# Prompt-tile heads issued one tile ahead, and a reordered end of the sample tile, in a hybrid DeltaNet / mLSTM encoder step

## What is computed

```python
# gated DeltaNet, per head, chunk by chunk
A = eye + where(strict, beta * (k @ k.T) * gam, 0)          # gam: decays between tokens
u_v, w = solve(A, [beta * v, beta * exp(G) * k])            # unit lower triangular
u = u_v - w @ S
o = exp(G) * (q @ S) + ((q @ k.T) * gam) @ u
S = exp(gL) * S + k_end.T @ u
o_a = o * rsqrt(mean(o * o) + EPS) * gdn_norm_w * silu(z_a)
# mLSTM, per head: stabilised, h = num / max(|den|, exp(-m))
h_b = h * rsqrt(mean(h * h) + EPS) * mlstm_norm_w * sigmoid(o_b)
x = x + concat([o_a, h_b]) @ w_out
```

## Time and profile before

| | us |
|---|---|
| median of 3 runs | 2611.95 (2611.59 to 2615.35) |
| the profiled execution | 2611.51, its span 2609.8 |
| PE busy in the span | 2564.2 (98%) |
| DVE busy | 2105.4 (81%) |
| ACT busy | 1213.3 (46%) |
| GpSimd busy | 355.2 (14%) |
| granted TensorE clock, mean | 0.995 |

### The profile page before, as it was taken

One profiled execution on the slowest core, in us unless ns is written; L12 is line 12 of the kernel. 1 busy time (PEld: TensorE's weight loads), 2 busy tenths in 40 slices (PEclk: granted clock), 3 DMA queues, 4 the chain that ended last, 5 costly groups with the idle time before them and its releaser, 6 DMA issues.

```text
span 2609.8 us, 43704 instructions
## 1 busy us (share of the span) xinstructions
PE 2564.2 (98%) x17600; PEld 2533.9 (97%) x17600; DVE 2105.4 (81%) x2614; ACT 1213.3 (46%) x1921; POOL 355.2 (14%) x186
## 2 busy tenths in 40 slices
PE   9999999998999999999999999999999999999998
PEld 9999999998999799999999999999999999999998
DVE  7979786887787889898877998988757788898756
ACT  5535454343444545455445554645311355454445
POOL 2200003332010120000024200000333300000042
PEclk9999999999999999999999999999999999999999
DMA  4223323232114423223323222223322222332231
GB/s 127 82 81 92 87 78 90 61 84 78 53 36 111 130 65 90 82 82 91 88 71 94 71 83 81 82 85 91 88 77 74 61 78 81 90 89 82 84 97 49
DMA packets 420251, 215.13 MB, mean 82 GB/s; under 512 B 19218, under 2 KB 418011, under 8 KB 420048
## 3 DMA queue, kind: packets, MB, share of 16 engines
q1 hardware_dynamic: 406066, 205.36, 27.6%
q10 hardware_dynamic: 13982, 6.96, 1.0%
HBM read 204.58 MB, written 7.68 MB: 81 GB/s over the span
## 4 chain that ended last, share of the span: by engine, by line
PE 56%; DVE 8%; ACT 2%; issue 1%; POOL 0%; DVEq 0%; ACTq 0%
PE ps L1124 13%; PE ps L1126 13%; PE ps L1125 13%; PE ps L1109 5%; PE ps L1110 5%; PE ps L1113 5%; PE ps L1182 1%; PE ps L1184 1%; PE ps L1183 1%; DVE sumsq L2666 1%; DVE ut L2561 1%; DVE x L3389 1%; DVE tau_lo L2630 1%; DVE r L2752 0%; DVE x L3574 0%
## 5 line engine op out<-in xcount | busy, mean ns | idle before, releaser
L1057 POOL TENSOR_TENSOR wlo<-raw,whi 128x1024 fp32r<-128x1024 f32 (+2 forms) x150 | 339.7, 2266 | 2215.9 <-ACT whi L1852 2215.9
L1124 PE MATMUL ps<-tau_hi,whi 128*128 128x320 f32 x1280 | 396.2, 309 | 0.5 <-ACT sq L2090 0.5
L1125 PE MATMUL ps<-tau_lo,whi 128*128 128x320 f32 x1280 | 395.9, 309 | 0.0
L1126 PE MATMUL ps<-tau_hi,wlo 128*128 128x320 f32 x1280 | 395.9, 309 | 0.0
L1863 ACT CAST whi<-raw 128x512 fp32r<-128x512 f32 (+4 forms) x368 | 258.1, 714 | 195.3 <-PE ps L1126 189.3
L1109 PE MATMUL ps<-xh,whi 128*128 128x320 f32 x1040 | 317.0, 313 | 4.2 <-POOL wlo L1057 2.3
L1110 PE MATMUL ps<-xl,whi 128*128 128x320 f32 x1040 | 313.4, 309 | 0.0
L2577 DVE TENSOR_TENSOR wlo<-raw,whi 128x512 fp32r<-128x512 f32 (+4 forms) x368 | 289.4, 801 | 17.3 <-ACT whi L1863 17.1
L1109 PE MATMUL ps<-hh,whi 128*128 128x320 f32 x928 | 282.4, 312 | 4.4 <-DVE hl L3018 2.1
L1110 PE MATMUL ps<-hl,whi 128*128 128x320 f32 x928 | 280.3, 310 | 0.0
L2577 DVE TENSOR_TENSOR wlo<-wsum,whi 128x1536 fp32r<-128x1536 f32 (+2 forms) x112 | 180.8, 1614 | 81.8 <-ACT whi L1863 80.3
(11 more groups left out here) (498 smaller groups left out, 6120.0 us busy)
## 6 DMA issues: line engine op xcount, KB each, us to landing
raw<-in_ffn_w_gu SPq DMA_DIRECT2D x320, 256.0 KB, 3.8
raw<-in_ffn_w_d SPq DMA_DIRECT2D x96, 192.0 KB, 3.0
raw<-in_w_in_even SPq DMA_DIRECT2D x32, 512.0 KB, 4.1
raw<-in_ffn_w_d SPq DMA_DIRECT2D x32, 384.0 KB, 3.6
raw<-in_w_in_odd SPq DMA_DIRECT2D x24, 512.0 KB, 3.8
raw<-in_ffn_w_gu SPq DMA_DIRECT2D x16, 512.0 KB, 4.3
raw<-in_ffn_w_d SPq DMA_DIRECT2D x64, 128.0 KB, 2.7
raw<-in_w_ple_gate SPq DMA_DIRECT2D x16, 512.0 KB, 4.1
```

The lines of the kernel that those rows point to most:

```text
L1057: pool.tensor_tensor(ring(wlo, n), raw[:, slot, 0:kt, :], ring(whi, n).bitcast(fp32), ALU.subtract).then_inc(lo_ready, 1)
L1124: pe.matmul(out, whi[:, w], hi(i), start=(start and i == 0), stop=False, skip_group_check=True)
L1125: pe.matmul(out, whi[:, w], lo(i), start=False, stop=False, skip_group_check=True)
L1126: last = pe.matmul(out, wlo[:, w], hi(i), start=False, stop=(i == kt - 1), skip_group_check=True)
```

## The change

In the prompt tiles `keys(t + 1)` on PE, `decays(t + 1)` on ACT and `delta_head(t + 1)` on DVE are issued at the end of tile t, the decays into `V(2)` instead of `W(1)`. The mask of level 1 goes into `W(1)` instead of `G_b`. The query products and their masking (`query_weights`) move into level 1, the transposed keys' factor into level 2, the exponentials of the gates (`gate_exps`) into level 1. On ACT `prep` of a later block stands behind the copy of the last tile's outputs (in tile 0: behind `decays`), and the copies of the gate halves move. The fillers are spread anew (still 96 per tile), with some between the halves of levels 2 and 4, and other banks.

In the sample tile the heads are multiplied by their gates (`gate`) ahead of the norm factor (`normalise`); `o_sums(0)` goes ahead of `state_c(1)`, 12 unused products go, `state_s(3)` goes behind the second block's first half; `normalisers_out` moves ahead of `first_blocks`; ACT's `prep(z0 + 10)` goes behind the first four casts; DVE's order of additions, gates, factors and low parts is new, with `add_s(3)` last.

```diff
@@ -413,12 +412,14 @@
-        Z_HEAD, Z_KS, Z_RT = 4, 8, 8
-        Z_D = {1: 0, 2: 6, 3: 0, 4: 3, 5: 6, 6: 6}
-        Z_NEXT = {1: 7, 2: 2, 3: 8, 4: 4, 5: 2, 6: 8}
+        Z_HEAD, Z_KS, Z_RT, Z_U = 20, 8, 6, 3
+        Z_MID = {2: 2, 4: 2}
+        Z_D = {1: 3, 2: 2, 3: 0, 4: 3, 5: 6, 6: 7}
+        Z_NEXT = {1: 8, 2: 2, 3: 11, 4: 4, 5: 2, 6: 7}
+        Z_BANK = [5, 4, 5, 5]
         ml_pe, ml_act, ml_dve = sem("ml_pe"), sem("ml_act"), sem("ml_dve")
         ML_PE = "qk vt kin kt num den up0 up1".split()
-        ML_ACT = "gates qin floor vt kin kt den".split()
+        ML_ACT = "gates qin vt kin kt floor den".split()
         ML_DVE = "qk q out up0 up1".split()
@@ -1335,15 +1336,23 @@
                 pe.wait_ge(lo_ready, n + 1)
-            if half % 4 != 2 and half:
-                pe.wait_ge(z_out, half - (half % 4 == 3))
+            if half % 4 != 1 and half:
+                pe.wait_ge(z_out, half - (half % 4 == 2))
         w = [ring(whi, n), ring(whi, n), ring(wlo, n)][m % 3]
         xs = [xh_, xl_, xh_][m % 3]
-        last = pe.matmul(bank([5, 5, 4, 5][half % 4])[:, 0:HT], w[:, k], xs[:, k, cs], start=(m == 0), stop=(m == 23))
+        last = pe.matmul(bank(Z_BANK[half % 4])[:, 0:HT], w[:, k], xs[:, k, cs], start=(m == 0), stop=(m == 23))
         if m == 23:
...
     filled[0] += count
+def keys(t):
+    k = qkv[:, HA:2 * HA, tile(t)]
+    pe.wait_ge(core["prod"], t + 1)
+    pe.wait_ge(core["expin"], t + 1)
+    per_head(4, lambda h: k[:, h], lambda h: W(0)[:, h]).then_inc(core["kk"], 1)
 def delta_tile(s, filled, t):
@@ -1351,19 +1360,7 @@
         token_rows(0)
-    pe.wait_ge(core["prod"], t + 1)
-    pe.wait_ge(core["expin"], t + 1)
-    per_head(4, lambda h: k[:, h], lambda h: W(0)[:, h]).then_inc(core["kk"], 1)
-    if t:
-        mlstm_part(t - 1, "up1")
-    z_fill(s, filled, 24)
-    if t:
-        pe.wait_ge(core["up"], t)
-    per_head(3, lambda h: k[:, h], lambda h: q[:, h]).then_inc(core["np"], 1)
+        keys(0)
     z_fill(s, filled, Z_HEAD)
@@ -1377,11 +1374,15 @@
                 pe.wait_ge(core["xr"], half_at(t, l - 1, g))
-            c_l = G_b if l == 1 else W(1)
-            per_head(g, lambda h: c_l[:, h], lambda h: W(6)[:, h], which=TWO[g]).then_inc(core["m1"], 1)
+            per_head(g, lambda h: W(1)[:, h], lambda h: W(6)[:, h], which=TWO[g]).then_inc(core["m1"], 1)
+            if g == 0 and l in Z_MID:
+                z_fill(s, filled, Z_MID[l])
         if l == 1:
             pe.wait_ge(core["xt0"], t + 1)
+            if t:
+                mlstm_part(t - 1, "up1")
+        if l == 2:
             pe.wait_ge(core["np_read"], t + 1)
@@ -1401,6 +1402,12 @@
             per_head(g, lambda h: W(8)[:, h], lambda h: W(7)[:, h], which=TWO[g]).then_inc(core["d"], 1)
+        if l == 1:
+            if t:
+                pe.wait_ge(core["up"], t)
+            per_head(3, lambda h: k[:, h], lambda h: q[:, h]).then_inc(core["np"], 1)
         for part in {2: ["qk"], 3: ["vt", "kin"], 4: ["num"], 5: ["den"], 6: ["up0"]}.get(l, []):
@@ -1411,7 +1418,7 @@
     pe.wait_ge(core["rT"], t + 1)
-    pe.wait_ge(z_out, 4 * t + 3)
+    pe.wait_ge(z_out, 4 * t + 2)
     for h in range(HA):
@@ -1421,6 +1428,9 @@
     token_rows(t + 1)
+    z_fill(s, filled, Z_U)
+    if t < NTILE - 2:
+        keys(t + 1)
     pe.wait_ge(core["utok"], t + 1)
@@ -1528,35 +1538,38 @@
     sample_part("den")
+    o_sums(0)
     state_c(1)
     sample_part("nsum")
-    o_sums(0)
     state_s(0)
     state_c(2)
+    normalisers_out()
+    o_sums(HA)
     state_s(1)
-    o_sums(HA)
     state_c(3)
     state_s(2)
-    unused_products(bank(6)[:, 0:P], 12)
-    state_s(3)
+def normalisers_out():
+    pe.wait_ge(ms_dve, MS_DVE.index("n") + 1)
+    pe.transpose(bank(6)[0:HB, 0:P], pC[:, :, P], ident[:])
+    for h in range(HB):
+        last = pe.transpose(bank(7)[0:DECB, h * P:(h + 1) * P], stc[:, h, :, P], ident[:])
+    last.then_inc(n_moved, 1)
 def first_blocks(s):
...
     hidden = (h_ready, s["hbase"])
-    pe.wait_ge(ms_dve, MS_DVE.index("n") + 1)
-    pe.wait_ge(o_root, 2)
-    pe.transpose(bank(0)[0:HB, P:2 * P], pC[:, :, P], ident[:])
-    for h in range(HB):
-        last = pe.transpose(bank(1)[0:DECB, h * P:(h + 1) * P], stc[:, h, :, P], ident[:])
-    last.then_inc(n_moved, 1)
+    pe.wait_ge(states_done, 2)
     for k in range(HA):
         mm(n, hi, lo, first=hidden, part=(k, k + 1))
-    pe.wait_ge(states_done, 2)
+    pe.wait_ge(o_root, 2)
     mm(n + 1, hi, lo, part=(0, HA))
+    state_s(3)
     pe.wait_ge(c_added, HB)
...
@@ -2321,20 +2334,17 @@
             act.dma_start(V(2), row_at("floor", t)).then_inc(floor_loaded, 16)
-        def decays(t):
+        def decays(t, out):
             act.wait_ge(beta_G_loaded, 32 * (t + 1))
             act.wait_ge(core["expin"], t + 1)
-            if t:
-                act.wait_ge(core["o"], t)
             for h in range(HA):
-                own(act.activation(W(1)[:, h], G_b[:, h], ACT.Relu, scale=-1.0, bias=gcols[:, h:h + 1]).then_inc(act_own, 1), act_own)
-            act.activation(W(1), W(1), ACT.Exp, scale=-1.0).then_inc(core["gam"], 1)
+                own(act.activation(out[:, h], G_b[:, h], ACT.Relu, scale=-1.0, bias=gcols[:, h:h + 1]).then_inc(act_own, 1), act_own)
+            act.activation(out, out, ACT.Exp, scale=-1.0).then_inc(core["gam"], 1)
+        def gate_exps(t):
             if 0 < t < NTILE - 1:
-                act.copy(qkv[:, 16:16 + HA, (t - 1) * P:t * P], heads(2))
                 act.wait_ge(core["up"], t)
@@ -2342,29 +2352,36 @@
         load_gates(0)
-        load_floor(0)
+        decays(0, V(2))
         for t in range(NTILE - 1):
...
             li, l2 = (LVL - 1) * t, (LVL - 2) * t
+            if t:
+                act.wait_ge(core["o"], t)
+                act.copy(qkv[:, 16:16 + HA, (t - 1) * P:t * P], heads(2))
             prep(z0 + [2, 3, 5, 7][t])
-            decays(t)
-            z_copy(4 * t)
             for l in range(1, L):
...
                     act.copy(two(W(8), g), two(heads(g), g)).then_inc(core["m1c"], 1)
-                for part in {2: ["gates", "qin"], 3: ["floor", "vt", "kin"], 4: ["kt"], 6: ["den"]}.get(l, []):
+                if l == 6:
+                    z_copy(4 * t + 2)
+                for part in {2: ["gates", "qin"], 3: ["vt", "kin"], 4: ["kt"], 5: ["floor"], 6: ["den"]}.get(l, []):
                     mlstm_part(t, part)
                 if l == 1:
+                    gate_exps(t)
                     act.wait_ge(core["eg"], t + 1)
                     load_beta_G(t + 1)
-                    if t:
-                        act.wait_ge(ml_dve, ml(ML_DVE, t - 1, "out"))
-                        load_floor(t)
+                if l == 2:
+                    z_copy(4 * t)
+                if l == 3:
+                    act.wait_ge(core["np_read"], t + 1)
+                    load_floor(t)
                 if l == 4:
@@ -2373,13 +2390,14 @@
                     prep(z0 + [4, 6, 8][t - 1])
-            z_copy(4 * t + 2)
             act.wait_ge(core["rt"], t + 1)
...
             act.copy(W(1), heads(3)).then_inc(core["utok"], 1)
+            if t < NTILE - 2:
+                decays(t + 1, V(2))
             z_copy(4 * t + 3)
...
@@ -2468,28 +2489,27 @@
         act.wait_ge(core["utok"], t + 1)
+        o_roots(0)
+        o_square(HA)
         spread_correction(1)
-        o_roots(0)
         spread_state(3)
-        o_square(HA)
-        prep(z0 + 10)
         spread_correction(2)
+        act.wait_ge(n_moved, 1)
+        act.copy(nout[0:HB, 0:P], bank(6)[0:HB, 0:P]).then_inc(states_done, 1)
+        act.copy(nout[0:DECB, P:], bank(7)[0:DECB, :]).then_inc(states_done, 1)
         o_roots(HA)
-        spread_correction(3)
         def o_cast(q):
-            if q % HA == 0:
-                act.wait_ge(o_gated, q + HA)
+            act.wait_ge(o_scaled, q + 1)
             act.copy(hh[:, q, :], qkv[:, 16 + q, :]).then_inc(o_high, 1)
...
             o_cast(q)
-        act.wait_ge(n_moved, 1)
-        act.copy(nout[0:HB, 0:P], bank(0)[0:HB, P:2 * P]).then_inc(states_done, 1)
-        act.copy(nout[0:DECB, P:], bank(1)[0:DECB, :]).then_inc(states_done, 1)
+        prep(z0 + 10)
+        spread_correction(3)
         for q in range(HA, 2 * HA):
@@ -2789,16 +2809,22 @@
     dve.wait_ge(core["kk"], t + 1)
-    mul(W(4), heads(4), W(1))
+    mul(W(4), heads(4), V(2))
+    if t:
+        dve.wait_ge(core["u"], t)
     mul(W(7), W(4), over_heads(level[:, 0, :]))
...
     own(dve.transpose(flat(6), flat(7)).then_inc(core["x0"], 1), core["x0"])
-    dve.wait_ge(core["eg"], t + 1)
-    own(dve.tensor_tensor(G_b[:], W(4), over_heads(level[:, 1, :]), ALU.mult).then_inc(core["ctl"], 1), core["ctl"])
+    if t:
+        dve.wait_ge(core["o"], t)
+    masked(1, (LVL - 1) * t)
+def query_weights(t):
     dve.wait_ge(core["np"], t + 1)
-    own(dve.tensor_tensor(W(5), heads(3), W(1), ALU.mult).then_inc(core["np_read"], 1), core["np_read"])
```

(67 more changed lines are left out.)

## The result

The changed kernel takes 2618.49 us, the median of 12 runs (2616.45 to 2623.03), against 2611.73 for 12 runs of the kernel before: 1.003 of the time, with a 95% interval of 1.0022 to 1.0037. It is slower by 6.8 us. The profiled execution of after took 2621.22, 2.7 above its median, and that of before 2611.51, at its median: traces differ by 9.7 us, some 3 more than the medians. At most 3.4 us of it are the clock, half of the 6.8 us that after has more at the lower level: between 635 us and the third update of x, TensorE runs for 23.9 us at a granted clock of 1.2 GHz in after and for 17.1 in before.

The account below looks back on a forecast made before the run. Neither engine alone was taken to bound a prompt tile: some 22.76 us of DVE's chain, then 20.07 of PE's work. Held heads, tile 0 and `up0` gave +5.9, the end -0.4: +5.5, 2617.4 us; range 2609 to 2622, sums' error 2614.5 to 2620.5.

Parts of the forecast that it names:

- The sum: Whole kernel: +5.9 before the sample tile and -0.4 at its end make +5.5 us, 2617.4 against the median.
- The three errors: Error of the sum: +-1 for tile 0, +-1.5 for three tiles, +-1.5 for the end, giving 2614.5 to 2620.5.
- Tiles without GpSimd, nothing won: Prompt tiles: covered PE wait comes back as waits for DVE, 42.87 us a tile against 42.83.
- rival (b): Prompt tiles and end: unseen DVE slack removes PE's waits and the store comes in time, 2604; chance 0.13.
- The mask of level 1 held: Prompt tiles: GpSimd's weight subtraction holds mask 1 by 1.41 us; three heads pay 4.35 in all.
- the 0.3 of `up0`: Tile before the sample tile: a new PE wait of 0.3 us at `up0`, as ACT copies a z half first.
- rival (a): Prompt heads: not held, or little, since GpSimd falls beside mask 1; 2610.5, chance 0.20.
- The first tile: Tile 0: GpSimd holds DVE's subtraction, so level 1 starts later; +1.7-0.4 = +1.3 us.
- rival (c): Three prompt tiles: PE's new waits make the clock fall, 3 x 2 = 6 us slower still, 2623; chance 0.14.
- The sample tile's end: Sample tile's end: PE's 4 us won are given back by the store wait; -1.1 to +0.3, taken as -0.4.
- rival (d): Sample tile's end: store wait doesn't exist or is passed in time, 2 us less, within the range; no separate chance.

Follow-up runs that it names:

- e3: Changed kernel with the four weight-unit casts (`prep`) on ACT put ahead of the decays again, in the first and later tiles: 2612.21 us, ratio 1.0007.
- e5: Changed kernel with the weight unit moved ahead of the next tile's decays for the later tiles only, first tile left as changed: 2616.99 us, ratio 1.0019.
- e10: Kernel before with the heads made ahead (as e1) and the weight units ahead of the decays (as e3), old sample end: 2610.80 us, ratio 0.9997.
- e8: Changed kernel with only SyncE's store order changed, so that one store is behind the last addition: 2616.75 us, ratio 1.0018.
- e9: Kernel before with the new sample end (as e2) and SyncE's stores reordered so that one is behind the last addition: 2610.93 us, ratio 1.0000.
- e12: Kernel before with only SyncE's new store order: 2611.64 us, ratio 1.0003.
- e2: Kernel before with only the change's new order of the sample tile's end, prompt tiles as before: 2611.23 us, ratio 1.0000.
- e7: Kernel before with only the weight unit moved behind the decays in tiles 2 to 4, no heads made ahead: 2613.32 us, ratio 1.0009.
- e6: Changed kernel with the weight unit moved ahead of the decays in the first tile only: 2616.32 us, ratio 1.0015.
- e1: Kernel before with only the change's heads of the prompt tiles made ahead, sample tile's end as before: 2617.06 us, ratio 1.0023.

## Why the prediction held, step by step

**The sum.** +5.5 forecast, +6.8 measured; 2617.4 against 2618.49, inside 2614.5 to 2620.5. (The three errors behind that range, 1, 1.5 and 1.5, add up to 4.0, or to 2.3 if they are independent; the 3 that it takes is neither.) The terms, by the runs that isolate them:

- *Tiles without GpSimd, nothing won*: right. 42.87 forecast, 43.02 in e3 to e5. That DVE's chain and PE's work meet at level 4 was read from the earlier trace rows; rival (b) needed a slack there. In e10, where neither hold nor end plays a part, the median is 1.0 under that of before, and its interval takes in zero.
- *The mask of level 1 held*: right in kind and size. Forecast 1.41, from 0.69 to an end 0.5 behind GpSimd; measured 2.19 - 0.69 = 1.50. Period 44.46 for 44.28; three periods +4.53 (1.64, 1.63 and 1.26) for 4.35 and the 0.3 of `up0`, which did not come: the last period grew least. The start of GpSimd was forecast 6.1 us behind `token_rows` and was 6.21 (691.28 - 685.07), the mask's 6.92 and was 6.95. The margin of 0.8 us that rival (a) had to beat was 0.74, the same in three tiles.
- *The first tile*: +1.3 forecast. From one `token_rows` to the next, e8, without a second fall, takes 48.36 us, and the four kernels with the old first tile and as much time at 1.2 GHz (6.8 us) 46.59 to 47.11 (e9, e12, e2, e7): +1.2 to +1.8. The profiled after is 1.6 longer still. That is what rival (c) describes, in a place where it wasn't put: behind PE's wait of 2.05 us, the clock fell again at 650.1 for 3.4 us. That the wait brings the fall is not shown, as e8 has the longer wait and no fall. In the later tiles, where (c) was put, the same wait of 1.7 us made no fall (granted clock 1.00).
- *The sample tile's end*: -0.4 forecast, with a range of -1.1 to +0.3. The median of e2, -0.3, can't tell; its trace has x(2) 0.67 later than before, counted from the sample tile's `token_rows`, with as much time at 1.2 GHz; e3 against e10 has 1.34 so, after against e12 1.38, e6 against e7 2.22. The mechanism held: what PE won was given back by the store wait, and rival (d) is out. But the size was 1.1 to 2.6 us too good. Set to before's start of the sample tile (e2's is 0.57 sooner), e2 has x(1) at 912.9 and x(2) at 920.8, for 911.2 to 912.4 and 919.0 to 920.4. PE's first product of the projection comes at 889.1, for 887.6, since GpSimd held the first low part and not the second:

```profile
885.35 2.35 POOL L1056 TENSOR_TENSOR wlo<-raw,whi 128x1024 fp32r<-128x1024 f32 x1 [18.95 <-ACT whi L1854]
...
885.42 2.96 DVE L3023 TENSOR_TENSOR hl<-qkv,hh 128x640 fp32r<-128x640 f32 x1
```

  And the store wait ended 6.1 us behind the last addition in e2, where 4.7 had been taken; of the 5.9 in after, 3.6 are SP's issue of four stores (from 913.40 to 917.00), the two small ones alone 2.5.
- *What was not in the sum*: the profiled after has +2.7 from the sample tile to x(2), for -0.4. It has 10.2 us at 1.2 GHz there and before has 6.8. Against e12, which has the old end and 10.2 us too, +1.4 are left for the end. By e1 and e2 the whole change is +5.2, and measured it is +6.8; the 1.6 between stay open, as medians of these kernels can't tell them. The time came within 1.1 us of the forecast although the end's term missed its own range; the range of the sum hid that.

**The rule behind the hold.** A DVE product with two SBUF inputs that starts inside a GpSimd subtraction of 128x1024 ends 0.55 us (128x512) behind it, in after, e7 and e8 alike; the reciprocal, the transposes and the products that read PSUM keep their times. The copy of squares has one SBUF input only and was held too, from 0.49 to 1.66 us. The Trainium skill, "SBUF — State Buffer", section "SBUF: two separate sides", says that the two engines take one port pair in turn and hold it for a whole instruction. The trace agrees: 2.19 us, and not the 1.4 at most that a shared bandwidth would give.

## What to carry to other kernels

When an instruction is moved on one engine's queue, look for what it releases on a third: here the order of PE and DVE was right, and a weight unit of ACT that slid some 4 us with it (GpSimd starts 6.2 us behind `token_rows`, and not 2.1) put GpSimd over the one DVE product that PE waits for. The same unit costs nothing over a reciprocal or a transpose and 1.5 us over a product of two SBUF tiles. And before an end is shortened on its bounding engine, read what the next stage waits for besides it, semaphores that count every store included: the last addition may go late only if little stands behind it in the store queue. Compare traces of small edits only where they have as much time at the lower clock.

## What the runs showed of the hardware

The granted clock of TensorE has two levels here, 2.4 and 1.2 GHz, and the same kernel with small edits has from 3.4 to 20.5 us at the lower one between the sample tile's start and x(2). The same 749 products of that stretch took from 109.31 to 114.24 us by that. Some falls came behind a wait of TensorE: at 650.1 in after, behind 2.05 us, and at 878.8, inside the wait of 3.11 us. But the 3.04 of e8, at the same place as the 2.05, was followed by no fall, nor were the waits of 1.7 in the later tiles. And some came with TensorE at work: in after the clock fell at 865.2, and in the 11.9 us up to 864.9 TensorE was busy all the time, as the window shows.

```profile
853.00:864.90 11.90, 11.90 (x98) 10.94 (x98) 11.52 (x12) 9.27 (x26) 0.00 (x0) 1.00 0.01 2
```

What decides over a fall was not settled. What it costs is as large as most of the edits tried here.
